# A fused two-block kernel: the second mixer's 64x64 inverse in longer runs of small products, with weight steps moved around it

## The reference, cut to what matters

```
def step(state, inp):
    r_t, w_t, k_t, v_t, a_t, b_t = inp
    sa = einsum('bhvk,bhk->bhv', state, a_t)
    state = state * w_t[:, :, None, :] + sa[..., :, None] * b_t[:, :, None, :] + v_t[..., :, None] * k_t[:, :, None, :]
    y_t = einsum('bhvk,bhk->bhv', state, r_t)
...
p = h @ w_in
y_a = rwkv7_mixer(p_rwkv, ...) @ rwkv_proj
y_b = fox_mixer(p_fox, ...) @ fox_proj
x = x + (sigmoid(gates_a) * y_a + sigmoid(gates_b) * y_b) @ w_out
```

## Time and profile before

| | |
|---|---|
| median of 3 runs | 1121.75 us (1121.33 to 1121.91) |
| profiled execution, its own time | 1122.1 us |
| span of its instructions | 1120.3 us |
| TensorE matmul busy | 1106.4 us, 99% |
| VectorE, ScalarE, GpSimd busy | 772.2, 580.1, 277.4 us |
| inverse, first L608 to first L677 | from 756.15 to 799.62 us |

### The profile page before, as it was taken

How to read it: one execution, slowest core, us unless ns; L and a number is a source line. 1 busy time by engine, 2 the same in 40 slices (tenths; PEclk the granted TensorE clock), 3 DMA queues, 4 the chain that set the end, 5 groups by cost and what they waited for, 6 DMA issues and landing times.

```text
span 1120.3 us, 20567 instructions
## 1 busy us (share of the span) xinstructions
PE 1106.4 (99%) x8778; PEld 1011.8 (90%) x8778; DVE 772.2 (69%) x1033; ACT 580.1 (52%) x703; POOL 277.4 (25%) x167
## 2 busy tenths in 40 slices
PE   9999999999999999999999999999999999999997
PEld 9999989999999999888888889999899989888886
DVE  4888978757787767776456467984378675564565
ACT  6433344594765545575445448622244656454454
POOL 3888883000000000003313330113030002233132
PEclk9999999999999999999999999999999999999999
DMA  8586553355466555535565564423134444655651
GB/s 273 190 278 213 188 188 113 113 183 187 142 196 208 187 187 187 188 128 188 193 204 180 192 193 152 147 77 115 41 114 151 149 155 152 223 176 193 212 173 52
DMA packets 143051, 189.96 MB, mean 170 GB/s; under 512 B 7659, under 2 KB 123947, under 8 KB 142847
## 3 DMA queue, kind: packets, MB, share of 16 engines
q1 hardware_dynamic: 141647, 184.32, 50.0%
q0 software_dynamic: 1264, 4.55, 1.2%
q10 hardware_dynamic: 64, 0.02, 0.0%
HBM read 187.79 MB, written 2.65 MB: 170 GB/s over the span
## 4 chain that ended last, share of the span: by engine, by line
PE 92%; DVE 4%; ACT 2%; issue 1%; DMA 1%; SPq 0%; ACTq 0%; DVEq 0%
PE banks L2261 14%; PE banks L2313 13%; PE banks L2262 13%; PE banks L2263 13%; PE banks L2318 7%; PE bank L2431 6%; PE bank L2432 6%; PE bank L2433 6%; PE bank L608 2%; DVE w_lo L1821 1%; PE bank L677 1%; DVE bank L2063 1%; PE bank L2263 1%; PE bank L2262 1%; PE bank L2261 1%
## 5 line engine op out<-in xcount | busy, mean ns | idle before, releaser
L1496 ACT ACTIVATE w_hi<-w_raw 128x2048 fp32r<-128x2048 f32 x170 | 324.0, 1909 | 93.2 <-PE banks L2263 68.3
L1821 DVE TENSOR_TENSOR w_lo<-w_raw,w_hi 128x2048 fp32r<-128x2048 f32 x144 | 336.0, 2337 | 41.0 <-ACT w_hi L1496 40.6
L2261 PE MATMUL banks<-X_both,w_hi 128*128 128x256 f32 x1120 | 321.3, 287 | 0.6 <-DVE w_lo L1821 0.5
L2262 PE MATMUL banks<-X_both,w_hi 128*128 128x256 f32 x1120 | 316.8, 283 | 0.0
L2263 PE MATMUL banks<-X_both,w_lo 128*128 128x256 f32 x1120 | 316.8, 283 | 0.0
L2261 PEld LDWEIGHTS banks<-X_both,w_hi 128*128 128x128 f32 x1120 | 214.5, 191 | 5.3 <-issue 2.6
L2262 PEld LDWEIGHTS banks<-X_both,w_hi 128*128 128x128 f32 x1120 | 214.5, 192 | 0.5
L2263 PEld LDWEIGHTS banks<-X_both,w_lo 128*128 128x128 f32 x1120 | 214.5, 192 | 0.0
L2313 PE MATMUL banks<-X_both,w_hi 128*128 128x512 f32 x640 | 201.0, 395 | 0.2 <-DVE w_lo L1821 0.2
L1433 POOL TENSOR_TENSOR arena<-arena,rstd 128x512 f32<-128x512 f32 x20 | 65.4, 3270 | 502.6 <-DVE arena L1954 502.6
L2318 PEld LDWEIGHTS banks<-X_both,w_lo 128*128 128x128 f32 x640 | 120.2, 188 | 28.2
(11 more groups left out here) (334 smaller groups left out, 1553.1 us busy)
## 6 DMA issues: line engine op xcount, KB each, us to landing
w_raw<-in_ffn_w_dram SPq DMA_DIRECT2D x66, 1024.0 KB, 5.2
w_raw<-in_w_in_dram SPq DMA_DIRECT2D x52, 1024.0 KB, 5.1
w_raw<-in_w_up_dram SPq DMA_DIRECT2D x22, 1024.0 KB, 5.0
w_raw<-in_w_down_dram SPq DMA_DIRECT2D x11, 1024.0 KB, 5.0
w_raw<-in_w_out_dram SPq DMA_DIRECT2D x8, 1024.0 KB, 5.0
w_raw<-in_conv_pw_w_dram SPq DMA_DIRECT2D x4, 1024.0 KB, 4.9
w_raw<-in_w_attn_out_dram SPq DMA_DIRECT2D x2, 1024.0 KB, 5.1
w_raw<-in_rwkv_proj_dram SPq DMA_DIRECT2D x2, 1024.0 KB, 4.8
```

The lines of the kernel that those rows point to most:

```text
L1496: a.activation(w_hi[slot][:, :], raw[slot][:, :], ACT.Copy).then_inc(S["w_hi"], told.one("w_hi"))
L1821: v.tensor_tensor(w_lo[slot][:, :], raw[slot][:, :], w_hi[slot][:, :].bitcast(F32), ALU.subtract).then_inc(S["w_lo"], told.one("w_lo"))
L2261: pe.matmul(o, wh, xh, start=start, stop=False, skip_group_check=True)
L2262: pe.matmul(o, wh, xl, start=False, stop=False, skip_group_check=True)
```

## The change

`first_product` of half 1 writes bank 0 (that of chunk B_FOX + 3, `first_bank`) instead of bank 4 at levels 1 to 4, so it no longer waits for the copy of half 0's P1 at once; at level 1 half 1 waits instead until VectorE has read chunk B_FOX + 3 out of bank 0. All steps of that chunk run ahead of the inverse. Inside the inverse no weights stand between level 1 and level 2, nor between level 3 and level 4; a whole value chunk stands after level 2 and after level 4, two steps of B_GA before the last second product and two behind it. ScalarE's and VectorE's splits of B_FOX + 5, + 6, + 7 move behind levels 2 and 4, VectorE's last one behind level 5.

```
+        def first_bank(n, f):
+            return bank_of[B_FOX + 3] if f and n < LEVELS else 4
...
-            columns(B_FOX + 3, steps=(1, 4))
+            columns(B_FOX + 3, steps=(1, NT))
...
-                if done > 0:
-                    pe.wait_ge(S["p1_copied"], done)
                 if n > 1:
+                    pe.wait_ge(S["p1_copied"], done if n == LEVELS else done - 1)
                     pe.wait_ge(S["x_added"], done - 1)
-                product(4, n_of, x_of, f).then_inc(S["p1"], told.one("p1"))
+                elif f == 1:
+                    pe.wait_ge(S[f"bank{bank_of[B_FOX + 3]}_read"], reads[B_FOX + 3])
+                product(first_bank(n, f), n_of, x_of, f).then_inc(S["p1"], told.one("p1"))
...
-            for n in range(1, LEVELS + 1):
+            first_product(1, 0)
+            first_product(1, 1)
+            second_product(1, 0)
+            for n in range(2, LEVELS + 1):
                 first_product(n, 0)
-                if n == 1:
-                    columns(B_FOX + 3, steps=(4, 5))
-                else:
-                    second_product(n - 1, 1)
-                if n == LEVELS:
-                    values(1, steps=(2, 3))
+                second_product(n - 1, 1)
                 second_product(n, 0)
                 first_product(n, 1)
-                if n == 1:
-                    columns(B_FOX + 3, steps=(5, NT))
-                elif n < LEVELS:
-                    values(n // 4, steps=(0, 2) if n != 3 else (2, 4))
-                else:
-                    values(1, steps=(3, 4))
+                if n % 2 == 0:
+                    values(n // 2 - 1)
+            columns(B_GA, steps=(0, 2))
             second_product(LEVELS, 1)
-            columns(B_GA, steps=(0, 1))
+            columns(B_GA, steps=(2, 4))
...
-                    columns(B_GA, steps=(1, 2))
+                    columns(B_GA, steps=(4, 5))
...
-            columns(B_GA, steps=(2, 3))
+            columns(B_GA, steps=(5, 6))
...
-                columns(B_GA + k, steps=(0 if k else 3, NT))
+                columns(B_GA + k, steps=(0 if k else 6, NT))
...
             dve.wait_ge(S["turned_copied"], 8)
+            out_bank(B_FOX + 3, fk[:, 2:4, :])
             for n in range(1, LEVELS + 1):
                 grow(n, 0)
-                if n in (1, 2, 4):
-                    split(B_FOX + (5, 6, 6, 7)[n - 1])
-                if n == 1:
-                    out_bank(B_FOX + 3, fk[:, 2:4, :])
+                if n == 2:
+                    split(B_FOX + 5)
+                if n == 4:
+                    split(B_FOX + 6)
                 grow(n, 1)
+            split(B_FOX + 7)
```

More of the change, by code:

```diff
@@ L877, in act_mixer @@
                     act.wait_ge(S["p1"], 2 * (n - 1) + f + 1)
-                    a.activation(half_1[:, f, :], bank[4][:, :], ACT.Copy).then_inc(
+                    a.activation(half_1[:, f, :], bank[first_bank(n, f)][:, :], ACT.Copy).then_inc(
                         S["p1_copied"], told.one("p1_copied"))
-                if n in (1, 2, 4):
-                    split(B_FOX + (5, 6, 6, 7)[n - 1])
+                if n == 2:
[3 more added lines that the diff above has]
+                    split(B_FOX + 7)
             v_tokens()
```

## The result

| | before | changed |
|---|---|---|
| median, 14 runs of each on the same chip | 1121.82 us (1121.33 to 1122.61) | 1124.57 us (1123.76 to 1125.18) |
| span of the profiled execution | 1120.3 us | 1122.8 us |

A forecast was written before the change was run, and what follows sets the result against it. TensorE was taken to bound the kernel (92% of the chain that ended last); -1.57 + 1.09 + 0.16 + 0.57 = +0.25 us on the profiled 1122.1 gave 1122.35, a median of 1122.0 us, range 1120.6 to 1123.4.

The forecast's parts named there:

- term 1: TensorE's borders between small-product runs and weight blocks, before the loop over c: fewer of them gain 1.57 us.
- term 2: Level 2's first product waits for VectorE's add of level 1's sum: 1.09 us of TensorE idle.
- term 3: Level 4's first product waits for VectorE's add with one product between: 0.16 us; other products have cover.
- term 4: Bank 0's wait, P1's copy, GpSimd's mask and the moved splits with their loads: all covered, costing nothing.
- term 5: Head norms: with gate steps moved ahead, k = 1's head sums wait for ScalarE's square, 0.57 us.
- term 4(d): Moved splits fit their cover; SyncE's delayed loads of B_GA + 2 to + 4 still come in time: no cost.
- rival B: Inverse: the 0.15 and 0.19 border times return within runs, so no gain: +1.82, 1123.6 us; chance 7%.
- The spread of k = 2: Head norms: VectorE's reciprocal ends at 836.64, TensorE reaches this spread at 837.37, so no wait.
- Term 4(a) to (c): Inverse: emptying bank 0 (no margin, at worst 0.68 us), ScalarE's copy of P1 and GpSimd's mask are hidden.
- Rival A: VectorE's add hands over sooner and the square isn't late, so only borders count: 1120.2 us; chance 9%.
- Rival C: Exposed adds and bank 0's scaling on VectorE stretch beside GpSimd's mask: +2.8 on the sum, 1124.8 us; chance 4%.
- Rival D: TensorE's clock falls from 2.4 to 1.2 GHz in level 2's new wait, costing 5.6: 1127.6 us; chance 2%.

The follow-up runs named there:

- Experiment 1: Changed kernel with SyncE's load of B_GA + 2 held until level 4's second first product, B_GA + 3's until the loop over c ends: 1122.58 us.
- experiment 2: Kernel before, with SyncE's load of B_GA + 1 waiting until GpSimd has made level 2's masks: 1124.02 us, 1.0018 of before.
- experiment 3: Changed kernel with two warm-up groups at its start replaced by small matmuls, 144 more instructions: 1122.83 us, 1.0012 of before.
- experiment 5: Kernel before, with the value steps at levels 2 to 4 cut in two, giving three more borders: 1123.03 us, 1.0010 of before.
- experiment 7: Changed kernel with two weight loads held back and B_GA's gate steps where they were before the change: 1121.84 us, 1.0002 of before.
- experiment 4: Changed kernel with only one warm-up group of 6 matmuls replaced by 32 small ones, 104 more instructions: 1123.53 us, 1.0015 of before.

## Why the prediction was wrong

The sum was +0.25; +2.75 came. Start to start in the trace of the changed kernel, part by part:

| | forecast | read |
|---|---|---|
| term 1, borders | -1.57 | -1.46 (4 x 0.145 + 0.185 + 3 x 0.23) |
| term 2, level 2's first product | +1.09 | +1.23 |
| term 3, other first products | +0.16 | +0.33 |
| term 4, what cost nothing | 0 | +1.98 |
| term 5, second head sums | +0.57 | +0.56 |
| sum | +0.25 | +2.64 |

The sum of the parts is within 0.1 of the 2.69 by which the two traces differ and of the 2.75 of the medians.

**The step that failed is term 4(d)**, "SyncE's loads of B_GA + 2 to + 4 wait for the moved splits and start up to 18 us later ... over ten us of cover". It asked only whether the weights come in time, and they do. It never asked what the transfers hold up while they run. In the kernel before, the blocks of weight steps between short runs gave a late block its time; in the changed kernel one load runs from 775.41 to 778.97 and another from 793.21 to 796.75, each over a long run of small products, and TensorE's own next instructions queue behind them. Experiment 1 takes the 1.98 away without touching TensorE's list, experiment 2 puts 1.6 into a kernel that didn't have it, and experiment 3 removes it by a shift of the instructions. It needed the long runs too, which come from the very merging that term 1 counts as pure gain. One of the prediction's own signs shows it: the loop over c was to start at about 801.5 and starts at 803.63.

**Term 1** was right to 0.1, and experiment 5 confirms it by itself; rival B falls. **Term 2** was right in its mechanism: the run of ten products lasts from 758.81 to 769.52, 10.71 where 10 x 0.933 + 0.145 = 9.48, so 1.23 more. VectorE's add ends at 763.62 and the product starts 0.15 later. Of the extra 0.14 this restart is 0.09: the prediction took 0.06 from a weight load in the loop over c. The rest isn't resolved. **Term 3** was right in size and wrong in number. In experiment 1's trace, where no pause hides it, the run of 12 and the run of 5 are each 0.17 over 0.933 a product + 0.145. The second is level 5's: "Every other product of a run has at least two products ... ahead of it" overlooked that level 5's second product is a single one. With a pause in the same run the first of them vanishes, so that 1.98 is counted against experiment 1. **Term 5** was right: from the spread of k = 0 to k = 1's head sums it takes 1.65 us (824.75 to 826.40) where it took 1.10 (822.90 to 824.00), and experiment 7 recovers 0.5. ScalarE's square ends at 826.35 and the sums start 0.05 later, so the 0.06 holds here. The spread of k = 2 has its cover, as forecast: its reciprocal ends at 840.01 and the spread starts at 841.43. **Term 4(a) to (c)** hold: bank 0, the copy and the masks show no wait.

**Rival A** (waits don't show) falls by term 2. **Rival C** gave 1124.8, close to what was measured, and is wrong: the adds take 0.69 as before. A number hit by another mechanism is no support. Beside a row of GpSimd one of VectorE's splits in the head norms does take 4.18 us instead of the mean 2.33 (before, one took 5.50), but TensorE doesn't wait there. **Rival D**: the granted clock is 1.00 in the stage.

The page of the Trainium skill cited in the prediction, "TensorEngine Tiling (Array Packing)", section Performance Considerations, has emptying PSUM as the limit of small tiles; here that rule costs 1.23 + 0.33, and the larger loss lies elsewhere. The span's 0.99 of TensorE hid all this: a list that is never idle has its own supply to be looked at.

## What to carry to other kernels

A load is not free because its data come early enough: while 1 MB is on its way (about 3.5 us), the compute engine's next instruction block (here TensorE's) may stand behind it. Where an engine runs long stretches of short instructions (here 64 in 0.93 us), keep large transfers out of them, or keep slower instructions between; and read idle time that the profile puts down to "issue" in the middle of a group of equal instructions beside the instruction queue in the DMA view. Before trusting a gain of 0.1%, shift the program by some hundred instructions: here that alone took 1.9 us out of the part from 239 us on, twice.

## What was not expected of the hardware

- TensorE's program arrives during the run, in blocks of 16.4 KB, 256 records apart, and late when a weight transfer is under way: 1.89, 2.71, 2.85 and 2.75 us after an edge in the four pauses seen, where 0.15 to 1.30 is usual. TensorE resumed 2.50 to 2.57 after the block's start in all four. A transfer doesn't always hold a block up: in experiment 4 one starts at 751.05, in the midst of weights that pass from 749.83 to 754.65. What decides it is not known.
- 144 or 104 instructions more at the start of the program changed a stage 750 us later by 1.98 us in the traces. The timing between copies of one kernel that differ only there is thus worth less than its interval says.
- After one wait TensorE's matmuls start 0.15 after the releasing engine's end (763.62 to 763.77), after another 0.05 (826.35 to 826.40), as its weight load in the earlier trace rows does after 0.06. Why they differ isn't known.
